# One VectorE instruction of 2048 columns in place of two of 1024 for the lower parts of a plain group's weights

## What is computed

```python
proj = _rms(x, norm1_g) @ w_in          # 2048 -> 7 * 1024 + 8 + 3 * 2048 columns
...
g = jax.nn.sigmoid(gate_logit).reshape(b, s, N_BRANCHES, D_MODEL)
merged = g[:, :, 0] * o_conv + g[:, :, 1] * o_fox + g[:, :, 2] * o_mem
x = x + merged @ w_out
h2 = _rms(x, norm2_g)
x = x + jnp.square(jax.nn.relu(h2 @ w_up)) @ w_down      # D_FF = 8192
```

## Time and profile before

| | |
|---|---|
| device time, median of 3 runs | 1623.67 us (1623.13 to 1623.91) |
| span of the profiled execution, first to last instruction | 1621.0 us |
| granted TensorE clock, mean over the span | 1.000 |
| TensorE matmuls busy | 1614.0 us, 100% of the span, 7406 instructions |
| VectorE busy | 1182.3 us, 73%, 1301 instructions |
| ScalarE busy | 872.5 us, 54%, 1025 instructions |
| HBM read | 312.59 MB, 194 GB/s over the span |

### The profile page before, as it was taken

How to read it: one execution, slowest core, us unless ns; L and a number is a source line. 1 busy time by engine, 2 the same in 40 slices (tenths; PEclk the granted TensorE clock), 3 DMA queues, 4 the chain that set the end, 5 groups by cost and what they waited for, 6 DMA issues and landing times.

```text
span 1621.0 us, 19990 instructions
## 1 busy us (share of the span) xinstructions
PE 1614.0 (100%) x7406; PEld 1341.8 (83%) x7406; DVE 1182.3 (73%) x1301; ACT 872.5 (54%) x1025; POOL 4.8 (0%) x13
## 2 busy tenths in 40 slices
PE   9999999999999999999999999999999999999998
PEld 8888888888888888888888888888888888888887
DVE  5877767555477777766665678887788787887877
ACT  6855444443455555544345566655665466556663
POOL 0000000000000000000000000000000000000000
PEclk9999999999999999999999999999999999999999
DMA  9766565555665666676556656566565656666654
GB/s 327 278 189 186 165 194 156 157 169 163 176 180 183 206 196 191 192 265 197 185 189 191 208 186 194 179 209 197 191 198 183 212 179 196 202 202 192 192 189 149
DMA packets 150134, 315.91 MB, mean 195 GB/s; under 512 B 9120, under 2 KB 9760, under 8 KB 149280
## 3 DMA queue, kind: packets, MB, share of 16 engines
q1 hardware_dynamic: 150048, 314.72, 61.6%
HBM read 312.59 MB, written 2.10 MB: 194 GB/s over the span
## 4 chain that ended last, share of the span: by engine, by line
PE 94%; DMA 2%; DVE 1%; ACT 1%; issue 1%; SPq 0%; DVEq 0%; ACTq 0%
PE bank L1996 42%; PE bank L1809 36%; PE bank L2099 9%; PE bank L2017 3%; DMA raw<-in_w_mem_kv 2%; PE bank L1828 2%; DVE wlo L1120 1%; ACT whi L647 1%; PE bank L1843 1%; PE bank L1948 0%; PE bank L1870 0%; PE bank L1910 0%; PE bank L1969 0%; DVE sm L1181 0%; DVE junk L1180 0%
## 5 line engine op out<-in xcount | busy, mean ns | idle before, releaser
L1120 DVE TENSOR_TENSOR wlo<-raw,whi 128x1024 fp32r<-128x1024 f32 x490 | 594.6, 1225 | 323.4 <-ACT whi L647 319.8
L647 ACT ACTIVATE whi<-raw 128x1024 fp32r<-128x1024 f32 x490 | 515.0, 1058 | 518.2 <-PE bank L1809 252.0
L1809 PE MATMUL bank<-whi,lhs_a 128*128 128x512 f32 x1280 | 397.3, 392 | 0.0
L1996 PE MATMUL bank<-whi,lhs_a 128*128 128x512 f32 x1248 | 385.3, 390 | 0.0
L1809 PEld LDWEIGHTS bank<-whi,lhs_a 128*128 128x128 f32 x1280 | 238.0, 188 | 47.7
L1996 PEld LDWEIGHTS bank<-whi,lhs_a 128*128 128x128 f32 x1248 | 233.8, 188 | 48.2
L1809 PE MATMUL bank<-wlo,lhs_a 128*128 128x512 f32 x640 | 249.5, 390 | 0.0
L1996 PE MATMUL bank<-wlo,lhs_a 128*128 128x512 f32 x624 | 243.1, 390 | 0.0
L1996 PE MATMUL bank<-whi,lhs_b 128*128 128x512 f32 x768 | 237.5, 391 | 0.0
L1996 PEld LDWEIGHTS bank<-whi,lhs_b 128*128 128x128 f32 x768 | 143.6, 188 | 29.4
L1996 PE MATMUL bank<-wlo,lhs_b 128*128 128x512 f32 x384 | 149.6, 390 | 0.0
(11 more groups left out here) (257 smaller groups left out, 1629.3 us busy)
## 6 DMA issues: line engine op xcount, KB each, us to landing
raw<-in_w_in SPq DMA_DIRECT2D x208, 512.0 KB, 3.8
raw<-in_w_up SPq DMA_DIRECT2D x96, 512.0 KB, 3.8
raw<-in_w_down SPq DMA_DIRECT2D x96, 512.0 KB, 4.5
raw<-in_w_out SPq DMA_DIRECT2D x32, 512.0 KB, 4.2
raw_f<-in_w_up SPq DMA_DIRECT2D x16, 1024.0 KB, 4.9
raw_f<-in_w_down SPq DMA_DIRECT2D x16, 1024.0 KB, 5.0
raw<-in_w_mem_kv SPq DMA_DIRECT2D x30, 512.0 KB, 6.3
raw<-in_w_conv_out SPq DMA_DIRECT2D x16, 512.0 KB, 4.6
```

The source lines that it names most:

```text
L647: act.activation(whi[n % RING], raw[slot], ACT.Copy).then_inc(hi_ready, 1)
L1120: dve.tensor_tensor(wlo[n % RING], raw[plain(n) % RING], whi[n % RING].bitcast(F32), ALU.subtract).then_inc(lo_ready, 1)
L1809: last = pe.matmul(dst, lhs[:, part, k + kk, s], w[:, kk, :], start=(k + kk == 0 and i == 0), stop=(k + kk == tiles - 1 and i == 2))
L1996: last = pe.matmul(bank[2 * side + tok], lhs[:, part, PK * k + kk, P * tok:P * (tok + 1)], w[:, kk, :], start=(at + kk == 0 and i == 0), s ...
```

## The change

VectorE gets a function `split_two` that waits until the upper parts of both pieces of a group are there, and then writes both lower parts with one instruction of 2048 columns, which adds 2 to `lo_ready`. It replaces the two instructions of 1024 columns in four plain groups of each of the 5 gate blocks (at 0, 3, 4 and 6) and, in every quarter of the MLP, in the groups at 1, 2, 3 and 5 of block 0, at 0, 2, 3, 5 and 6 of blocks 1 and 2, and at 0, 3, 4, 6 and 7 of block 3: 20 and 76, 96 in all. Where other work stands between the two halves (`left` and `right`), they stay as they are. What was hung on side 0 of a group (`wo_events`, `conv_events`) now follows behind both. The lists of the other engines do not change.

```diff
+            def split_two(n, base=0):
+
+                r, slot = n % RING, plain(n) % RING
+                dve.wait_ge(hi_ready, base + (n + 2))
+                dve.tensor_tensor(wlo_all[:, r:r + 2, :], raw_all[:, slot:slot + 2, :],
+                                  whi_all[:, r:r + 2, :].bitcast(F32), ALU.subtract).then_inc(lo_ready, 2)
+
...
             def gate_lower(at, jb, sides=(0, 1)):
+                if len(sides) == 2:
+                    split_two(gate_piece(jb, at))
+                else:
+                    split(gate_piece(jb, at) + sides[0])
                 for side in sides:
-                    split(gate_piece(jb, at) + side)
                     conv_events(gate_piece(jb, at) + side)
...
-                def lower(blk, at, sides=(0, 1)):
-                    for side in sides:
-                        split(ff_piece(q, blk, at) + side, base=by_n)
-                        if q == 0:
+                def one_side(blk, at, side):
+                    split(ff_piece(q, blk, at) + side, base=by_n)
+                    if q == 0:
+                        wo_events(ff_piece(q, blk, at) + side)
+
+                def lower(blk, at):
+                    split_two(ff_piece(q, blk, at), base=by_n)
+                    if q == 0:
+                        for side in range(2):
                             wo_events(ff_piece(q, blk, at) + side)
...
                 def left(blk, at):
-                    lower(blk, at, (0,))
+                    one_side(blk, at, 0)
```

More of the change, by code:

```diff
@@ L1645, in quarter @@
                 by_n, by_b, by_8, by_f = i * FF_PIECES, i * FF_BLOCKS, i * (2 * FF_BLOCKS), i * FASTS
-                def lower(blk, at, sides=(0, 1)):
-                    for side in sides:
-                        split(ff_piece(q, blk, at) + side, base=by_n)
-                        if q == 0:
+                def one_side(blk, at, side):
[6 more added lines that the diff above has]
+                        for side in range(2):
                             wo_events(ff_piece(q, blk, at) + side)
                 def left(blk, at):
-                    lower(blk, at, (0,))
+                    one_side(blk, at, 0)
                 def right(blk, at):
-                    lower(blk, at, (1,))
+                    one_side(blk, at, 1)
                 def fast(blk, at):
```

## The result

The changed kernel takes 1647.25 us, median of 5 runs (1644.24 to 1649.24), against 1623.13 us for the kernel before in the same job: 1.0149 of its time, 95% interval 1.0138 to 1.016. It is slower by 24.1 us, with 96 VectorE instructions less. The prediction said 1640.3 and a range up to 1645.5; its direction holds, its size doesn't. The profiled execution is the fastest of the five, 1644.24 us with a span of 1642.1, so that its trace explains 21.1 us and not 24.

A forecast was written before the change was run, and what follows sets the result against it. The prediction took TensorE, with one matmul about every 0.227 us, as the limit. Its terms, 9.4 + 3.3 + 3.1 + 0.3 + 0.5 = 16.6 us, added to 1623.7 gave 1640.3 us, range 1634 to 1645.5.

The forecast's parts named there:

- A: Group 6 of MLP blocks 1 and 2, 8 places: TensorE waits 1.21 us each for side 0, 9.4 us in all.
- B: Block 3, fast group at 5, 4 places: VectorE 0.88 us later, TensorE waits 0.86 us, 3.3 us in all.
- C: Start of the MLP, once: addition to `x_sb` ends later, TensorE waits 2.35 and 0.74 us, 3.1 us together.
- Loads: SyncE's ring reloads, 3.8 us later for side 0: costed at nothing, hidden by the distance to their next use.
- late loads on top: Rival, 12%: paired reloads at gates' block starts and quarters' starts cost 1 us at each of 4 + 3 places, 1647 us.
- D: Gates' fast group at 5, 5 places: VectorE's last part 0.88 us later, 0 to 0.11 us each, 0.3 in all.
- E: Start of quarters 1 to 3: VectorE 0.88 us late, TensorE waits 0.17 us three times, 0.5 us.
- Sum and span: Whole kernel: terms add 16.6 us, span 1621.0 becomes 1637.6, the median stands 2.7 us above the span.
- The page's rule: VectorE, 96 pairs: 162 ns less busy each; read alone, the rule would promise a gain of up to 15.6 us.

The follow-up runs named there:

- only_a: The kernel before with one instruction for both lower parts only at the group at 6 of MLP blocks 1 and 2 (8 pairs): 1637.52 us (1.0087).
- only_b: The kernel before with one instruction for both lower parts only at the group at 4 of block 3 (4 pairs): 1626.35 us (1.0018).
- only_c: The kernel before with one instruction for both lower parts only at groups 1 to 3 of the MLP's first block (3 pairs): 1627.06 us (1.002).
- late_release: The kernel before, all instructions kept, but SyncE waits for both lower parts before loading either place again: 1623.45 us (0.9999).
- after_thin: The changed kernel with block 2's two ring loads ahead of block 3's 1 MB load cut from 512 to 16 columns: 1645.83 us (1.0125 to 1.0155).
- after_load_first: The changed kernel, loads whole, with the 1 MB load for block 3's fast group at 2 issued ahead of the two ring loads: 1645.78 us (1.0117 to 1.0147).
- gate_3_single: The changed kernel with pairs in the gates alone, at 0, 4 and 6; the group at 3 has two instructions again: 1625.1 us (1.0011).
- after_again: The changed kernel, unaltered, run and profiled a second time: 1647.7 us (1645.12 to 1650.45).

## Why the prediction was wrong

**What bounds it, and the mechanism: right.** TensorE was the limit, VectorE's saving was worth nothing, and the cost is TensorE waiting for side 0. only_a, only_b and only_c show each of A, B and C by itself.

**The step that failed: Loads.** "I cost this at nothing; what hides it is that distance." The distance was real, and in late_release a release late by one piece costs nothing in the median. But I counted only the loads of the late places themselves. The two that start together are still streaming when the 1 MB load behind them is issued, and that one lands up to 3 us late, at a fast group, where VectorE has no slack. The trace before showed that: VectorE's sums wait there for the landing already, ten times in the kernel.

```profile
DVE t_raw L1537 <- DMA raw_f<-in_w_down: 9.1, 10, 1.2
```

And the 3.8 us of the earlier trace rows are those of `w_up`; the same page has 4.5 us for the loads of `w_down`, which these are. In the median the late load is some 1.5 us in the changed kernel by the runs that remove it at one place (up to 3.6 on top of A alone), and by the traces 1.4 and 3.5 us over both such places. The prediction held the price (*late loads on top*, up to 1 us each, 1647 us), but put it at the starts of blocks and quarters, where I found 0.1 to 0.8 us at one place, the fast group at 2 of the gates' first block; that its time fits is in part chance, since A, C and D gave their share.

**What else the sum lacked.** Loads are not the whole miss: after_thin and after_load_first still stand 22.6 us above the kernel before, and 16.6 were forecast. The trace of after_thin accounts for the difference: A 1.2 us more than its term, B 0.4, C 1.1 (of it 0.9 the clock), D 0.9, E 0.3, another late load 1.5, the start 0.5. TensorE's clock was a term at nothing too. The prediction read a granted clock of 1.000 over the kernel before and priced each wait by its length and 0.11 us, and the wait of 2.3 us that it forecast at C brought the clock to 0.50 in five traces of seven.

**Term A** was mis-sized: 10.5 us for 9.4, 1.25 to 1.4 a place and not 1.21. The instruction's length and the 0.11 us for the first two matmuls are as computed. But it starts 0.11 us behind ScalarE's end, not 0.04: 1006.48 in the row above, where side 1's upper part ended at 1005.33 + 1.04 = 1006.37:

```profile
1005.33 1.04 ACT L647 ACTIVATE whi<-raw 128x1024 fp32r<-128x1024 f32 x1
```

So TensorE starts 1.19 us late, not 1.10. It is so at all pairs that wait for ScalarE: 0.10 us in the median of 73 such starts, against 0.03 for the 167 of L1120. It could have been read ahead. In the trace before, the lower part of 1536 columns in the earlier trace rows starts at 558.10, and the upper part that it waits for ends at 556.53 + 1.47 = 558.00:

```profile
556.53 1.47 ACT L849 ACTIVATE whi<-raw 128x1536 fp32r<-128x1536 f32 x1
```

All 22 starts of this form that wait for ScalarE have 0.10 us there. The prediction had taken its 2288 ns from `t_lo`, which is as long, and whose four waiting starts have 0.03.

**Term B** was right but for this: 3.6 us alone, 0.91 a place and not 0.86. In the changed kernel it is 3.2, since in quarter 0, where TensorE had lost time to the late load just before, only 0.54 was left of it.

**Term C** was right in its chain and a little short: 2.6 and 0.7 us in the profiled execution, where 2.35 and 0.74 were forecast. The 4.2 us of five other traces are the lower clock, above. The rows show the first wait:

```profile
939.29 2.29 DVE L1127 TENSOR_TENSOR wlo<-raw,whi 128x2048 fp32r<-128x2048 f32 x1 [5.01 <-ACT whi L647]
...
941.73 0.70 PE L2011 MATMUL bank<-whi,lhs_b 128*128 128x512 f32 x2 [2.31 <-DVE wlo L1127]
```

**Term D** failed by a factor: 2.1 us for 0.3. In part it is size (0.2 us in each block in after_thin and in gate_3_single, where 0.06 was taken). The sums start 0.08 us behind the pair's end and not 0.09 ahead of it, as in block 1 of the gates in the changed kernel (551.26 + 2.29 = 553.55):

```profile
551.26 2.29 DVE L1127 TENSOR_TENSOR wlo<-raw,whi 128x2048 fp32r<-128x2048 f32 x1 [3.41 <-ACT whi L647]
553.63 1.23 DVE L1448 TENSOR_TENSOR gt_raw_a<-raw 128x1024 f32<-128x1024 f32 x1
```

The rest of D, most of it in one block or two, is late ring loads once more, the step above, and 0.2 us at the first block's fast group at 2. **Term E** was a little short, 0.8 for 0.5.

**Sum and span.** The five terms gave 16.6 where the trace has 19.9; the loads add 1.4 to 3.5. The profiled execution took 2.1 us more than its span (1644.24 to 1642.1), and it was the fastest of five; the median lies 3.0 us above it. The second trace has 3.0 us of late loads and clock that the first lacks, besides 2.9 at the start. A forecast of the median from one trace has no place for what comes in some executions only.

**The page's rule.** The Trainium skill, "VectorE: DVE Perf Modes", section on the TRN2 errata, has a fixed latency paid once for each instruction. By the means it is 2 x 1225 - 2291 = 159 ns a pair. VectorE's busy time fell by 9.3 us over 96, 97 ns a pair: where two splits ran without a gap they overlapped, 2.36 us for both, and only 0.07 us were saved.

## What to carry to other kernels

Join two instructions only where their inputs become ready together and nobody waits for the first half. Then compute, at each place, when the first reader wants that half; the mean idle time says nothing (VectorE was idle 27% of the span and cost 20 us). A joint release also joins the loads behind it: look not only at whether they land in time, but at which big load is issued while they still stream, and put that one ahead of them. And price a wait of TensorE of some 2 us apart from the short ones, for it can take the clock along.

## What the runs showed of the hardware

- At block 3's fast group at 2 a 1 MB load lands in 4.8 to 5.1 us in the kernel before, with the engines quiet ahead of it, and in up to 8.2 with two 512 KB loads streaming up to its issue: the bulk is as fast, a tail of 18 to 37 GB/s is late (in the changed kernel one of 16 increments, at 7.5 us). Loads issued right behind it don't do that (4.8 to 5.1 us in the two kernels with this load first). Quiet engines are no guarantee: 5.9 us once in only_c. A few other 1 MB loads are late in every kernel, the one before too (8.0 us at the first block's fast group at 4 of quarter 0); they are hidden there, and no run looked for their cause.
- A stall of TensorE costs more than its length: after 1.03 us of waiting the first two matmuls take 0.73 for 0.62 us.
- Behind the wait of 2.3 us at the start of the MLP the granted clock fell to 0.50 in five traces of seven, for some eight matmuls 0.43 us apart. Behind the 56 waits of about 1 us at A's places in seven traces it never fell; at the start of the kernel it fell behind one of 1.83 us in only_b and not behind one of 1.9 in after_again.
- VectorE starts the new instruction 0.10 us behind the end of ScalarE's, and so the lower parts of 1536 columns; the split of 1024 columns mostly 0.03 us behind it, and `t_lo` of 2048 columns too. So it isn't the size; no run tells whether operand shape or the wait makes it.
